# State-space layer: SiLUs behind an odd piece's first convolution, low gated values behind the last part's operands, output heads in alternating order

## The chip, the cores and the metric

The kernel runs on one core of a Trainium2 chip. The metric is the device time of the whole kernel in microseconds (us). Engines are called PE (TensorE), ACT (ScalarE), DVE (VectorE), POOL (GpSimd) and SP (SyncE). Each works through its own queue strictly in order, and they meet only at semaphores.

## What is computed

The reference is four stacked layers on 256 tokens (272 with 16 meta tokens) of width 1024. The change touches the mixer of the last one, a Mamba-2 state-space layer:

```python
proj = u @ w_in
z, xbc, dt = jnp.split(proj, [D_SSM, D_SSM + SSD_CONV_DIM], axis=-1)
xbc = jax.nn.silu(causal_dwconv(xbc, conv_w, conv_b))
...
y = ssd_chunked(front_pad(xs), front_pad(dt), a, front_pad(bs), front_pad(cs))[:, PAD:]
y = y + d_skip.astype(jnp.float32)[:, None] * xs
y = y.reshape(bsz, L, D_SSM) * jax.nn.silu(z.astype(jnp.float32))
yg = y.reshape(bsz, L, SSD_GROUPS, D_SSM // SSD_GROUPS)
yg = yg * lax.rsqrt(jnp.mean(yg * yg, axis=-1, keepdims=True) + EPS)
y = yg.reshape(bsz, L, D_SSM) * gate_norm.astype(jnp.float32)
return y.astype(u.dtype) @ w_out
```

There are 8 groups of 4 heads (head width 64, state 128). A group takes 4 tiles of 128 convolved channels (B, C and two of x) and 2 tiles of gate z.

## The kernel before

**Products.** Each weight is split into two f16 parts. SP loads a slot (two tiles of 128 columns) as f32; ACT writes its high part (`high_part`, L1538), DVE its low part (`low_part`, L2144), four slots ahead of use. In this layer each engine does half a slot behind each tile: tile j belongs to half (j-1) % 2. ACT signals `high_ready` only after the second half, so DVE's low part of a tile with an odd j waits until ACT has done the tile after it. A tile of the product is 24 matmuls (L690 to L692).

**Order of the layer's input product.** `mamba_pieces` deals the tiles into 16 pieces, two for each group g: piece s = 2g + k. Eleven tiles (j = 0 to 10) come before piece 0. Pieces 0 to 5 have two convolution tiles and a z tile; pieces 6 to 12 have two convolution tiles; pieces 13 to 15 have two z tiles. So the first tile of a piece has an even j in pieces 1, 3 and 5 and an odd j in pieces 7, 9, 11, 13, 14 and 15. In what follows A and B are the first and second tile of an odd piece, C and D those of the even piece after it.

- PE, odd piece: `first_outputs(g)` (L1423, L1424), `second_inputs(g)` (L1373 to L1364), A, `gate_sums` (L1446), B, a z tile if there is one. Even piece: `second_outputs(g-1)` (L1435 to L1437), `first_inputs(g)` (from L1384), C, `last_inputs(g)` (L1373 to L1398), D, a z tile if there is one. At the end `second_outputs(7)` and the product `out_m`, which waits for the release of all its four banks before it begins; the bank of tile 48 is one of them.
- ACT, odd piece: `second_exps` (L2069 to L2072), `silus` (a table load L2025, SiLU over the next group's four tiles L2028, SiLU over a pair of z tiles L2031 where one is due, a table load L2032), then for each tile its evacuation (L2019, for z L1524) and the high part (L1538), with `gate_squares` and `gate_root` (L2036, L2041, L2043) behind the first. Even piece: `first_exps` (L2057, L2059), `high_y` (L2047) where due, evacuation of C, `last_exps` (L2063 to L2065), `gate_squares`, evacuation of D. Pieces 14, 15 and the step after them (s = 16) call `silus` too, for the z pairs 5, 6 and 7.
- DVE: `outputs` (L2760), `weighted_x` (L2745), `scores` (L2751), low parts, three taps of each convolution (L2534), `gate_normed` (L2768), `low_y` (L2772).
- POOL, at even s: the gating y * silu(z) (L2974) of a pair that is due, which waits for that pair's SiLU; behind it `xw` (L2977), for which PE's `first_outputs` waits; `cd` (L2979); the squares' sum (L2983).

`GATES_AT` lists the steps s at which the pairs 0 to 7 are gated: 2, 4, 6, 8, 10, 14, 15, 16. `high_y` and `low_y` of a pair come two steps later. `first_inputs(g)` also waits for the `gate_root` of the piece before, since they share a bank.

Of the kernel before, what the change touches and what calls it, by code (L numbers as in the profile page):

```python
# [19 lines left out]
P = 128  # L20
# [12 lines left out]
META = 16  # L33
T = S + META
HD = 64
# [10 lines left out]
SSM_G = 8  # L46
SSM_HEADS = 32
SKIP = META - 2
REST = P + META
# [319 lines left out]
def two_stacks(nc, stream, small, params, consts, x_t, meta_t, out_t):  # L369
# [14 lines left out]
    with ExitStack() as ctx:  # L384
# [24 lines left out]
        def bank(b, lo=0, hi=512, rows=slice(0, P)):  # L409
            return psum[rows, b, lo:hi]  # L410
# [114 lines left out]
        xdt, xdt_c, xw = (sq_flat[:, 4 * HD * i:4 * HD * (i + 1)] for i in range(3))  # L525
# [156 lines left out]
        def _(pe):  # L682
# [665 lines left out]
            def mamba():  # L1348
                order, pieces = mamba_order(), mamba_pieces()
# [61 lines left out]
                def half_rows(h):  # L1411
                    return slice(64 * (h % 2), 64 * (h % 2) + 64)
# [13 lines left out]
                def second_outputs(g):  # L1426

                    pe.wait_ge(xdt_ready, 3 * g + 3)
                    pe.wait_ge(mt_ready, 3 * g + 3)
                    pe.wait_ge(y_out, 2 * g + 1)  # L1430
                    pe.wait_ge(prev_ready, g + 1)
                    pe.wait_ge(cd_ready, g + 1)
                    for h in range(4):
                        at, heads = (h // 2) * REST, slice(h * HD, h * HD + HD)
                        pe.matmul(bank(6, at, at + REST, half_rows(h)), xdt[:, heads], seg[:, h, :], start=True, stop=False)  # L1435
                        pe.matmul(bank(6, at + P, at + REST, half_rows(h)), xdt_c[0:META, heads], seg_c[0:META, h, :], start=False, stop=False)
                        mm = pe.matmul(bank(6, at, at + REST, half_rows(h)), prev[:, heads], cd[:, h, :], start=False, stop=True)  # L1437
                    mm.then_inc(y_done, 1)

                def gate_sums(g, s):  # L1440
# [75 lines left out]
        def _(act):  # L1516
# [481 lines left out]
            def mamba():  # L1998
# [89 lines left out]
                for s, piece in enumerate(pieces + [[], [], []]):  # L2088
                    g, k = divmod(s, 2)
                    if s < len(pieces):  # L2090
                        if k == 0:
                            first_exps(g)
                        else:
                            second_exps(g)
                    if s <= len(pieces) and (k or g + 1 >= SSM_G):
                        silus(g + 1 if k else SSM_G, range(gated, gates_in // 2))
                        gated = gates_in // 2
                    if s - 2 in GATES_AT:
                        high_y(GATES_AT.index(s - 2))
                    for i, (kind, _) in enumerate(piece):  # L2100
                        evac(j)
                        j += 1
                        gates_in += kind == "z"
                        if i == 0:
                            if k == 0:
                                last_exps(g)
                            gate_steps(s)
                    if not piece:
                        if s == len(pieces):
                            high_part(products["in_m"]["steps"][-1][0] + SPLIT)  # L2110
                        gate_steps(s)
# [20 lines left out]
        def _(dve):  # L2132
# [578 lines left out]
            def mamba():  # L2711
# [70 lines left out]
                for s, piece in enumerate(pieces + [[], [], []]):  # L2782
                    g, k = divmod(s, 2)
                    if 0 < s <= len(pieces):
                        outputs(s - 1)
                    if s < len(pieces):
                        weighted_x(3 * g + 2 * k, xdt, P, 2 * k)
                    if behind and k:
                        evac(behind)
                    if s < len(pieces):  # L2790
                        scores(3 * g + 2 * k, seg, P, REST if k else P)
                    if behind and not k:
                        evac(behind)
                    if behind:
                        behind_tile("in_m", behind)
                        behind = None
                    if s == len(pieces):
                        low_part(products["in_m"]["steps"][-1][0] + SPLIT)
                    if s - 2 in GATES_AT:
                        low_y(GATES_AT.index(s - 2))  # L2800
                    for i in range(len(piece)):
                        if i + 1 < len(piece):
                            evac(j)
                        if i == 0 and k == 0:
                            weighted_x(3 * g + 1, xdt_c, META, 3)
                            scores(3 * g + 1, seg_c, META, META)
                        if i + 1 < len(piece):
                            behind_tile("in_m", j)
                        else:
                            behind = j  # L2810
                        j += 1
                        if i == 0 and s - 1 in GATES_AT:
                            gate_normed(GATES_AT.index(s - 1))
                    if not piece and s - 1 in GATES_AT:
                        gate_normed(GATES_AT.index(s - 1))
# [321 lines left out]
```

## Time and profile before

| | |
|---|---|
| median of 3 runs | 1453.53 us (1453.22 to 1454.57) |
| profiled execution | 1452.95 us, its span 1451.2 us |
| PE busy | 1398.3 us (96%) |
| DVE busy | 1055.4 us (73%) |
| ACT busy | 833.0 us (57%) |
| POOL busy | 518.5 us (36%) |
| mean granted TensorE clock | 0.989 |

The profile is one execution. Times in its rows are us from the span's start, durations of one are in us in a timeline. The state-space layer's pieces run from about 1030 to 1211 us. A row of a timeline ends with the time for which the engine sat idle before it and what released it. The granted clock is given as a share: 1.00 is the 2.4 GHz level and 0.50 the 1.2 GHz level.

### The profile page before, as it was taken

The numbers are of one execution on the slowest core, as the hardware profiler recorded it, in microseconds if no ns is written. First come the engines' busy times: TensorE is split into PE (matmuls) and PEld (weight loads), VectorE is DVE, ScalarE is ACT, GpSimd is POOL, SyncE is SP. The second block draws the span as 40 slices with busy tenths as digits, with TensorE's granted clock in tenths as the row PEclk, the third lists the DMA queues.
The fourth block names the chain that finished last, engine by engine and source line by source line (L and its number), as shares of the span: only waits on it lengthen the run. The fifth ranks groups of instructions, "written<-read, shape, count | busy, mean of one in ns | idle before, by whom it ended". The sixth has DMA issues, their size and how long they took to land.

```text
span 1451.2 us, 29999 instructions
## 1 busy us (share of the span) xinstructions
PE 1398.3 (96%) x12859; PEld 1183.5 (82%) x12859; DVE 1055.4 (73%) x1361; ACT 833.0 (57%) x1253; POOL 518.5 (36%) x421
## 2 busy tenths in 40 slices
PE   8989999999899999999999999999999999999997
PEld 7778888888788888878678788887777778888886
DVE  5887986567797884567786888766667765898853
ACT  6575554337574453456885665545566777575552
POOL 0123995131047990234210366401212202146620
PEclk9989999999899999999999999999999999999998
DMA  9434466545323665525235355552533233556550
GB/s 369 172 117 146 148 212 213 191 163 182 127 100 117 231 206 203 189 88 189 93 133 212 137 200 180 189 193 88 174 113 121 86 107 118 200 185 206 189 177 30
DMA packets 35717, 235.61 MB, mean 162 GB/s; under 512 B 4736, under 2 KB 6784, under 8 KB 8832
## 3 DMA queue, kind: packets, MB, share of 16 engines
q1 hardware_dynamic: 35584, 233.68, 46.8%
q8 instruction: 102, 1.67, 0.5%
q14 instruction: 31, 0.25, 0.1%
HBM read 232.62 MB, written 1.05 MB: 161 GB/s over the span
## 4 chain that ended last, share of the span: by engine, by line
PE 76%; DVE 13%; ACT 7%; issue 2%; DMA 2%; SPq 0%; DVEq 0%; ACTq 0%
PE psum L690 23%; PE psum L692 23%; PE psum L691 23%; DVE low L2144 4%; PE psum L778 2%; DVE arena L2534 2%; ACT high L1538 2%; DMA raw<-stream 2%; ACT m L1891 1%; DVE m L2602 1%; PE psum L1044 1%; DVE arena L2605 1%; PE psum L1027 1%; ACT arena L2028 0%; ACT L2025 0%
## 5 line engine op out<-in xcount | busy, mean ns | idle before, releaser
L2144 DVE SCALAR_TENSOR_TENSOR low<-raw,high 128x2048 f16<-128x2048 f32 (+4 forms) x246 | 527.4, 2150 | 255.5 <-ACT high L1538 255.4
L690 PE MATMUL psum<-u,high 128*128 128x272 f16 (+3 forms) x2136 | 589.6, 276 | 14.7 <-DVE u L2445 5.4
L691 PE MATMUL psum<-u,high 128*128 128x272 f16 (+3 forms) x2136 | 589.1, 276 | 0.0
L692 PE MATMUL psum<-u,low 128*128 128x272 f16 (+3 forms) x2136 | 589.0, 276 | 0.0
L1538 ACT ACTIVATE high<-raw 128x2048 f16<-128x2048 f32 (+4 forms) x246 | 419.9, 1712 | 140.3 <-PE psum L692 125.8
L690 PE MATMUL psum<-arena,high 128*128 128x256 f16 (+2 forms) x1264 | 346.7, 274 | 2.8 <-ACT arena L1876 1.5
L692 PE MATMUL psum<-arena,low 128*128 128x256 f16 (+2 forms) x1264 | 346.6, 274 | 0.0
L691 PE MATMUL psum<-arena,high 128*128 128x256 f16 (+2 forms) x1264 | 346.6, 274 | 0.0
L690 PEld LDWEIGHTS psum<-u,high 128*128 128x128 f16 (+1 forms) x2136 | 209.9, 98 | 52.8 <-issue 15.6
L691 PEld LDWEIGHTS psum<-u,high 128*128 128x128 f16 (+1 forms) x2136 | 210.0, 98 | 31.1 <-issue 0.7
L692 PEld LDWEIGHTS psum<-u,low 128*128 128x128 f16 (+1 forms) x2136 | 209.8, 98 | 30.5
L2888 POOL TENSOR_TENSOR arena<-arena 128x256 f16<-128x256 f32 (+1 forms) x108 | 170.6, 1579 | 8.5
L2886 POOL TENSOR_TENSOR arena<-arena 128x256 f32<-128x256 f32 (+1 forms) x108 | 128.2, 1187 | 107.4 <-DVE arena L2550 105.7
L2534 DVE SCALAR_TENSOR_TENSOR arena<-psum,par,arena 128x271 f32<-128x271 f32 (+3 forms) x296 | 143.7, 492 | 23.3 <-ACT arena L2019 6.4
L690 PEld LDWEIGHTS psum<-arena,high 128*128 128x128 f16 x1264 | 123.7, 98 | 21.2 <-ACT arena L1876 1.8
L691 PEld LDWEIGHTS psum<-arena,high 128*128 128x128 f16 x1264 | 123.7, 98 | 18.4
L692 PEld LDWEIGHTS psum<-arena,low 128*128 128x128 f16 x1264 | 123.7, 98 | 16.5
L1524 ACT ACTIVATE arena<-psum 128x256 f32<-128x256 f32 (+3 forms) x138 | 51.7, 382 | 109.4 <-PE psum L692 68.8
L1839 ACT ACTIVATE arena<-psum,par 128x272 f32<-128x272 f32 (+1 forms) x88 | 49.4, 571 | 86.5 <-PE psum L692 85.0
L2896 POOL TENSOR_TENSOR m<-m,rstd 128x272 f32<-128x272 f32 (+1 forms) x12 | 9.0, 748 | 154.0 <-ACT rstd L1816 154.0
L2974 POOL TENSOR_TENSOR arena<-arena 128x516 f32<-128x516 f32 x8 | 11.2, 1395 | 117.3 <-DVE arena L2760 96.4
L2431 DVE TENSOR_TENSOR arena<-arena 128x256 f16<-128x256 f32 x64 | 48.4, 783 | 2.1 <-ACT arena L1524 2.1
(331 smaller groups left out, 1496.3 us busy)
## 6 DMA issues: line engine op xcount, KB each, us to landing
raw<-stream SPq DMA_DIRECT2D x208, 1024.0 KB, 4.8
raw<-stream SPq DMA_DIRECT2D x8, 768.0 KB, 4.2
raw<-stream SPq DMA_DIRECT2D x3, 896.0 KB, 5.1
con<-consts SPq DMA_DIRECT2D x1, 1758.0 KB, 16.7
raw<-stream SPq DMA_DIRECT2D x3, 512.0 KB, 3.5
h<-x_t SPq DMA_DIRECT2D x2, 512.0 KB, 6.2
out_t<-h SPq DMA_DIRECT2D x4, 256.0 KB, 2.1
misc<-small SPq DMA_DIRECT2D x1, 512.0 KB, 13.2
```

Source lines behind the costliest of these rows:

```text
L690: pe.matmul(out, w_hi, x[0], start=start, stop=False)
L691: pe.matmul(out, w_hi, x[1], start=False, stop=False)
L692: return pe.matmul(out, w_lo, x[0], start=False, stop=stop)
L778: return pe.matmul(bank(b, 0, n), C("mean", 0, P), x, start=start, stop=stop)
L1524: tell(act.activation(dst, bank(BANK[g], at, at + n, rows), func, scale=scale / W_SCALE), *evac_value(g))
L1538: tell(act.activation(high[:, at:at + w], raw[:, off:off + w], ACT.Copy, scale=W_SCALE), high_ready if half != 0 else None)
L1839: tell(act.activation(buf[:, i % GATED, 0:outputs], bank(BANK[g], ahead, ahead + outputs), ACT.Identity, scale=pcol(f"ffn_w{l}", 2 * 2 * F ...
L2144: tell(dve.scalar_tensor_tensor(low[:, at:at + w], raw[:, off:off + w], W_SCALE, high[:, at:at + w], ALU.mult, ALU.subtract), split_ready ...
L2431: tell(dve.tensor_tensor(f1_hi[:, t, :], f_relu[:, t % 4, :], f_relu[:, t % 4, :], ALU.mult), fh_ready)
L2534: ins = dve.scalar_tensor_tensor(dst[:, lo:outputs], bank(BANK[g], at, at + n), weight(taps_in_all - 1 - back), dst[:, lo:outputs], ALU.mu ...
L2886: tell(pool.tensor_tensor(tmp[:, t % 2, 0:n], a[:, t % depth, 0:n], b[:, t % depth, 0:n], ALU.mult))
L2888: tell(pool.tensor_tensor(lo[:, t, 0:n], tmp[:, t % 2, 0:n], hi[:, t, 0:n], ALU.subtract), f_ready)
```

## The change

Three edits, all in `mamba`. PE: in `second_outputs` the twelve products (each two instructions in the trace) are issued in two pairs of heads, the two heads of a pair alternating; the sums are the same. ACT: `silus` moves from ahead of the piece's tiles to behind the first tile's evacuation and high part (and behind `last_exps` in an even piece), for pieces 14 and 15 too; without a piece (s = 16) it stands behind `high_y`, which it preceded. DVE: `low_y`, where there is a piece, moves from ahead of C's taps to behind C's taps and the operands of the last part (`weighted_x` and `scores` of xdt_c, seg_c).

```diff
-                    for h in range(4):
-                        at, heads = (h // 2) * REST, slice(h * HD, h * HD + HD)
-                        pe.matmul(bank(6, at, at + REST, half_rows(h)), xdt[:, heads], seg[:, h, :], start=True, stop=False)
-                        pe.matmul(bank(6, at + P, at + REST, half_rows(h)), xdt_c[0:META, heads], seg_c[0:META, h, :], start=False, stop=False)
-                        mm = pe.matmul(bank(6, at, at + REST, half_rows(h)), prev[:, heads], cd[:, h, :], start=False, stop=True)
+                    for pair in ((0, 1), (2, 3)):
+                        at = (pair[0] // 2) * REST
+                        for h in pair:
+                            pe.matmul(bank(6, at, at + REST, half_rows(h)), xdt[:, h * HD:h * HD + HD], seg[:, h, :], start=True, stop=False)
+                        for h in pair:
+                            pe.matmul(bank(6, at + P, at + REST, half_rows(h)), xdt_c[0:META, h * HD:h * HD + HD], seg_c[0:META, h, :],
+                                      start=False, stop=False)
+                        for h in pair:
+                            mm = pe.matmul(bank(6, at, at + REST, half_rows(h)), prev[:, h * HD:h * HD + HD], cd[:, h, :], start=False, stop=True)
                     mm.then_inc(y_done, 1)
...
-                    if s <= len(pieces) and (k or g + 1 >= SSM_G):
-                        silus(g + 1 if k else SSM_G, range(gated, gates_in // 2))
-                        gated = gates_in // 2
                     if s - 2 in GATES_AT:
                         high_y(GATES_AT.index(s - 2))
+                    with_silus = s <= len(pieces) and (k or g + 1 >= SSM_G)
+                    if with_silus and not piece:
+                        silus(SSM_G, range(gated, gates_in // 2))
+                        gated = gates_in // 2
                     for i, (kind, _) in enumerate(piece):
                         evac(j)
                         j += 1
-                        gates_in += kind == "z"
                         if i == 0:
                             if k == 0:
                                 last_exps(g)
+                            if with_silus:
+                                silus(g + 1 if k else SSM_G, range(gated, gates_in // 2))
+                                gated = gates_in // 2
                             gate_steps(s)
+                        gates_in += kind == "z"
...
-                    if s - 2 in GATES_AT:
+                    if s - 2 in GATES_AT and not piece:
                         low_y(GATES_AT.index(s - 2))
                     for i in range(len(piece)):
...
                             weighted_x(3 * g + 1, xdt_c, META, 3)
                             scores(3 * g + 1, seg_c, META, META)
+                        if i == 0 and s - 2 in GATES_AT:
+                            low_y(GATES_AT.index(s - 2))
```

## Rows read from the trace of the kernel before

**Rows 1.** Windows: us, busy of PE, PEld, DVE, ACT, POOL; clock; DMA share; GB/s
```profile
1030.00:1213.00 183.00, 173.84 (x1578) 137.03 (x1577) 124.27 (x218) 124.08 (x200) 33.55 (x30) 0.99 0.34 113
1038.00:1039.00 1.00, 1.00 (x7) 0.70 (x6) 0.54 (x3) 0.77 (x3) 0.00 (x0) 0.50 0.99 418
80.00:85.00 5.00, 5.00 (x143) 3.99 (x142) 3.14 (x4) 4.11 (x12) 0.00 (x0) 0.67 0.69 228
85.00:92.00 7.00, 4.53 (x26) 3.27 (x23) 6.74 (x14) 2.50 (x5) 0.00 (x0) 0.50 0.73 272
```

**Rows 2.** Waits, 1030 to 1240 us: total us, times, longest us
```profile
DVE low L2144 <- ACT high L1538: 49.1, 17, 5.7
PEld psum L1436 <- issue: 6.3, 32, 0.2
PE psum L1373 <- DVE arena L2751: 7.0, 5, 2.7
```

**Rows 3.** Timeline of PE, pieces 5 and 6: start, us, engine, line
```profile
1101.45 0.60 PE L1446 MATMUL psum<-m,con 128*128 128x258 f32 x2
...
1115.55 0.20 PE L1373 MATMUL psum<-arena 128*16 128x16 f32 x2 [1.11 <-DVE arena L2751]
```

**Rows 4.** Timeline of ACT, piece 5
```profile
1100.75 1.28 ACT L2025 ACT_TABLE_LOAD   x1
...
1105.13 0.58 ACT L2019 ACTIVATE arena<-psum,par 128x272 f32<-128x272 f32 x1
...
1109.06 1.05 ACT L1538 ACTIVATE high<-raw 128x1024 f16<-128x1024 f32 x1
```

**Rows 5.** Timeline of DVE, piece 5
```profile
1106.69 1.23 DVE L2144 SCALAR_TENSOR_TENSOR low<-raw,high 128x1024 f16<-128x1024 f32 x1 [5.17 <-ACT high L1538]
...
1112.71 1.22 DVE L2144 SCALAR_TENSOR_TENSOR low<-raw,high 128x1024 f16<-128x1024 f32 x1
```

**Rows 6.** Timeline of ACT, piece 9 (two tiles)
```profile
1148.40 0.58 ACT L2019 ACTIVATE arena<-psum,par 128x272 f32<-128x272 f32 x1
...
1151.12 1.04 ACT L1538 ACTIVATE high<-raw 128x1024 f16<-128x1024 f32 x1
```

**Rows 7.** Timeline of DVE, piece 8 and the end of piece 9
```profile
1138.17 1.90 DVE L2772 TENSOR_TENSOR arena<-arena 128x516 f16<-128x516 f32 x1
...
1152.19 1.23 DVE L2144 SCALAR_TENSOR_TENSOR low<-raw,high 128x1024 f16<-128x1024 f32 x1 [1.61 <-ACT high L1538]
```

**Rows 8.** Timeline of PE: first matmul of `second_inputs` of groups 4, 5 and 6
```profile
1142.09 0.48 PE L1373 MATMUL psum<-arena 128*128 128x144 f32 x2 [1.02 <-DVE sq L2745]
...
1161.57 0.41 PE L1373 MATMUL psum<-arena 128*128 128x144 f32 x2
...
1182.34 0.48 PE L1373 MATMUL psum<-arena 128*128 128x144 f32 x2 [1.02 <-DVE sq L2745]
```

**Rows 9.** Timeline of ACT, pieces 14 and 15 and step 16
```profile
1193.91 1.28 ACT L2025 ACT_TABLE_LOAD   x1
...
1209.80 0.37 ACT L1524 ACTIVATE arena<-psum 128x258 f32<-128x258 f32 x1
...
1214.91 1.90 ACT L1538 ACTIVATE high<-raw 128x2048 f16<-128x2048 f32 x1
```

**Rows 10.** Timeline of POOL, piece 14: `xw`
```profile
1197.22 0.61 POOL L2977 TENSOR_TENSOR sq<-sq,arena 128x256 f32<-128x256 f32 x1
```

**Rows 11.** Timeline of PE, end of piece 14 to the start of `out_m`
```profile
1195.83 0.22 PE L1373 MATMUL psum<-arena 128*16 128x16 f32 x2
...
1199.70 0.66 PE L1423 MATMUL psum<-arena,sq 128*64 128x128 f32 x8
1200.28 0.70 PE L1424 MATMUL psum<-sq,arena 128*128 128x256 f32 x2
...
1207.85 0.46 PE L1435 MATMUL psum<-arena,sq 128*64 128x144 f32 x2
...
1210.67 0.28 PE L690 MATMUL psum<-arena,high 128*128 128x258 f16 x1
```

**Rows 12.** Timeline of DVE, step 16: low part of the fourth slot of `out_m`
```profile
1216.84 2.29 DVE L2144 SCALAR_TENSOR_TENSOR low<-raw,high 128x2048 f16<-128x2048 f32 x1 [1.98 <-ACT high L1538]
```

## Prediction

> **What bounds the kernel now.** The page says PE is busy 96% of the span, so the first view is the windows of the stage that the change touches: from 1030 to 1213 us PE is idle for 183.0 - 173.8 = 9.2 us [rows 1]. No reordering can win more there than this plus whatever PE work it removes. The second view is the waits: PE's largest is last_inputs (L1373) behind DVE's scores, 7.0 us in five waits, and DVE's own largest is its low part behind ACT's high part, 49.1 us [rows 2]. The third is the timelines of one round on three engines. The chain in piece 5 reads: ACT starts its SiLUs at 1100.75, although PE has tile A ready only at 1101.45 (gate_sums follows it); it reaches A at 1105.13 and ends the z tile's high part at 1109.06 + 1.05 [rows 3, 4]. DVE has sat 5.17 us for the high part that goes with A, and from there is busy without a break: the low part of B starts at 1112.71, and 2.8 us later PE's last_inputs is released, after an idle 1.11 us [rows 3, 5]. So DVE's late start, caused by ACT's order, is what PE waits for. Rounds of two-tile pieces are different. There the low part of A has an odd j and waits for the high part of B anyway (1152.19, behind ACT's 1151.12 + 1.04) [rows 6, 7], and what PE waits for is second_inputs, 1.02 us in two of three rounds, in which low_y took 1.90 instead of about 0.7 [rows 7, 8].
>
> **SiLUs behind A, pieces 1, 3 and 5.** ACT now waits for A: about 0.2 behind 1101.45, 0.9 later than its SiLUs start today. The work between is the same, so its last high part of the piece ends at 1110.11 + 0.9 = 1111.0. DVE's low part of the earlier tile starts four us sooner, its taps of A and B follow while ACT works, and its low part of B, which needs that last high part, starts at 1111.0 instead of 1112.71: 1.7 sooner. Everything from there to last_inputs is unchanged. That would release PE at 1113.85; C ends at 1115.55 - 1.11 = 1114.44 today and at 1113.5 with shorter output heads (below), so PE is still the earlier one. Three such rounds of the same pattern: **-5.1 us**. Of the 1.7, 1.1 is the idle time of today and 0.6 needs C to end sooner, which only the shorter heads bring.
>
> **SiLUs behind A, pieces 7, 9 and 11.** Here B's high part decides, and it is only delayed by ACT's wait for A. A loop forms: A ends, 0.2, ACT for 7.5 (evacuation and high part 1.4, SiLUs with two table loads 3.7, root 0.8, B 1.5), DVE for 3.5 (low part 1.1, gate_normed 0.8, outputs 0.55, weighted_x and scores 1.0), 0.1, PE for 9.1 (last_inputs 1.1, D 2.9, first_outputs 1.1, second_inputs 1.2, A 2.8): 20.4 us. Today a round from second_inputs to second_inputs is 19.5 (1142.09 to 1161.57) and 20.8 (1161.57 to 1182.34) [rows 8]. So the one round costs +1.0 and the other gains 0.4. The round before them (piece 7) enters from the three-tile regime: last_inputs is 0.9 later, but the 1.2 us around the wait at 1142.09 is gone, see low_y: -0.4. Together **+0.2 us**.
>
> **low_y behind the operands.** It no longer stands ahead of C's taps, so scores for second_inputs is ready up to 1.9 sooner. DVE then waits for D's high part in any case, and low_y fits in that wait of 1.3. This removes PE's two waits of 1.02, already used in the loop above. Nothing early waits for low_y itself (only out_m), so its own lateness costs nothing. Alone it is worth between 0 and -2.4.
>
> **Alternating heads.** second_outputs takes 1210.67 - 1207.85 = 2.82 us [rows 11]. The rows show heads of different halves running side by side: first_outputs, whose neighbours alternate, does eight instructions of 128 columns in 0.58 (1199.70 to 1200.28), and in second_outputs PE stalls 0.2 in front of each head's 16-row product (32 of them, 6.3 us) [rows 2, 11]. Alternating leaves 16 of these stalls and lets both long products overlap: 0.40 + 0.21 + 0.7 + 0.21 + 0.40 = 1.9, so 0.9 less for each group, 7.3 us in all; 0.4 if the short products don't overlap. On the path it is worth the 0.6 in each of three rounds that is counted above (C at 1113.5 instead of 1114.44, against DVE's 1113.85), and nothing elsewhere: in the other rounds C ends before DVE or ACT release what follows. The Trainium skill (TensorEngine Tiling (Array Packing), Key Properties) says that tiles of the array operate independently and that changing the mode drains the engine. By that rule each switch between 128 and 16 rows is a drain, and halving the switches would save about the amount above; the 0.2 us stalls agree. It changes nothing in the sum.
>
> **Piece 13** has z tiles: ACT waits 1.8 for its first tile, DVE's low part slips 1.9, and last_inputs(7) is bound by scores again. I take -0.3, between 0 and the heads' 0.9.
>
> **SiLUs in piece 14: a new wait.** POOL's gating waits for the SiLU of pair 5, and xw is queued behind it; PE's first_outputs(7) waits for xw. Today ACT starts that SiLU's table load at 1193.91, and xw is done at 1197.8, 1.9 ahead of PE's 1199.70 [rows 9 to 11]. Moved, the table load stands behind tile 45's evacuation, the whole of last_inputs (1195.83 + 1.13) and last_exps: 1195.83 + 1.13 + 0.2 + 0.8 = 1198.0, plus 1.28 + 0.63 of SiLU, 0.1, 1.24 of gating, 0.61 of xw, 0.1 = 1202.0. PE is ready at 1199.70: **+2.3 us**.
>
> **SiLUs in piece 15.** Today ACT evacuates tile 48 by 1209.80 + 0.37 = 1210.17, 0.5 ahead of out_m at 1210.67 [rows 9, 11], which waits for that bank. ACT's queue there is now: wait for tile 47 (it is ready at 1204.68), its evacuation and high part 1.2, SiLUs 3.2, squares and root 1.5, then tile 48. Counted from first_outputs(7), that bank is free 11.65 us on, against 10.97 today for out_m's start: **+0.7 us**; the 0.9 of shorter heads is lost in this wait.
>
> **Step 16.** high_y now stands ahead of silus and must wait for DVE's gate_normed, about 2.0 us behind tile 48's high part. That delays the fourth slot's high part (1214.91) and low part (done at 1219.05). Its margin: PE wants it 11.0 behind out_m's start, at 1221.7 [rows 9, 11, 12]. The margin of 2.6 is used up by 2.1 here and the rest of piece 15's lateness; I take 0, up to +0.5.
>
> **Sum.** -5.1 + 0.2 - 0.3 + 2.3 + 0.7 = -2.2 us. The profiled execution would go from 1452.95 to 1450.8, and the median, 0.6 above it, from 1453.53 to 1451.4. A measurement of this kernel can tell about 0.2%, 2.9 us, from no change; the forecast lies inside that.
>
> **Rivals.**
> *The tail waits don't arise* (chance 0.20): if POOL's xw or the bank of tile 48 has a slack that I misread, only the front counts: -5.1 to -5.3, 1448.4. Against it: both orders are fixed in the code and the margins are 1.9 and 0.5.
> *A short fall of the clock* (0.22): PE would idle 2.3 us ahead of first_outputs(7) and 1.6 ahead of out_m. After the longest wait of the stage, 2.7 us, the granted clock went from 1.00 to 0.50 (the 1.2 GHz level) [rows 1, 2] and about 3 us at it cost 1.4. After waits of 1.1 it did not. That gives -0.8, 1452.8.
> *Slower, by a long fall* (0.12): another fall held half clock through the 7 us of 85 to 92 and about a third of the 5 us before, some 10 us at half rate [rows 1]. If the waits in front of first_outputs(7) and out_m bring such a one while PE has nothing but out_m to do, it costs 5.1: +2.9 and more, 1456.5. It decides only if both waits come, since only then is PE twice idle in 10 us.
> *The heads don't overlap* (0.06), so the edit doesn't do what it says: second_outputs stays near 2.8. C would then be last in the three-tile rounds by 0.6 each: -0.4, 1453.1.
> *My forecast*: 0.40.
>
> The forecast's own range is 1450.4 to 1452.4. The 8-in-10 range leaves out the long fall and reaches the others: 1448.0 to 1454.0. Faster by over 0.2% takes the first rival and a third of the forecast, 0.34; slower 0.12; within 0.54.
>
> **What would show it.** Right: three low parts of DVE behind ACT at about 1 us instead of 5; last_inputs of groups 1 to 3 with idle time of 0.5 or less; L1435 to L1437 spanning 1.9 instead of 2.8; no idle before L1373 of second_inputs; an idle of about 2.3 before L1423 of group 7 put down to POOL's L2977, and one of 1.6 before out_m put down to ACT's L1524. Wrong: the round of piece 9 no longer than today, POOL's xw ahead of PE, or a granted clock of 0.50 near 1200.

## The result, and the profile after

| | before | after |
|---|---|---|
| median of 13 runs | 1453.8 us (1452.74 to 1455.38) | 1456.84 us (1452.0 to 1460.7) |
| profiled execution | 1452.95 us, span 1451.2 us | 1456.38 us, span 1454.6 us |
| mean granted clock | 0.989 | 0.986 |

The ratio is 1.002, 95% interval 1.0013 to 1.0027: the changed kernel is slower by about 3.0 us (1.9 to 3.9). The forecast was 1451.4, with 1448.0 to 1454.0 as its range. It was wrong in sign, and the time lies outside the range. One of the ten runs of experiment 7 took 2893.15 us; it is in no ratio, and without it the median there is 1452.79.

Lines have moved. ACT: L1538 is now L1542, L2019 is L2023, L2025 is L2029, L2031 is L2035, L1524 is L1528, and `gate_root`'s last line, L2043, is now L2047 (the number that `high_y` had before). DVE: L2144 is L2152, L2745 is L2753, L2751 is L2759. POOL: L2974 and L2977 are L2984 and L2987. PE's L1373, L1423 and L690 have kept their numbers, and L1435 to L1437 are now L1436 to L1441.

**Busy time.** The page of the changed kernel, each engine's busy time:

```profile
PE 1395.1 (96%) x12859; PEld 1181.5 (81%) x12859; DVE 1052.6 (72%) x1361; ACT 832.8 (57%) x1253; POOL 518.2 (36%) x421
```

PE is busy for 3.2 us less than before, and the kernel takes 3.4 us more in the profiled pair. So the alternating heads did remove work from the bounding engine. Where the time went is seen in the waits and in the clock.

**Waits.** PE, 1030 to 1250 us, changed kernel (total us, times, longest us):

```profile
PE psum L1373 <- DVE arena L2759: 7.5, 8, 2.7
PE psum L1384 <- ACT arena L2047: 4.5, 3, 1.9
PE psum L1423 <- POOL sq L2987: 2.4, 1, 2.4
PE psum L690 <- issue: 1.7, 1, 1.7
```

The third and the fourth row are the two tail waits of the forecast. The second is new and was not forecast: `first_inputs` of groups 4, 5 and 6 now waits for `gate_root` (ACT's L2047). ACT reaches it later, and PE is there sooner by its shorter heads. The first is the wait of [rows 2] for scores. It was 7.0 us in five waits and is now spread over eight. The waits at `last_inputs` of groups 1 to 3 fell from 1.27, 1.11 and 1.11 us to 0.67, 0.53 and 0.53. The 2.7 us of piece 0 is as before.

**The three-tile rounds.** ACT in piece 5, changed kernel (start, us, engine, line):

```profile
1099.59 0.58 ACT L2023 ACTIVATE arena<-psum,par 128x272 f32<-128x272 f32 x1 [0.93 <-PE psum L692]
...
1101.13 1.28 ACT L2029 ACT_TABLE_LOAD   x1
...
1108.02 1.05 ACT L1542 ACTIVATE high<-raw 128x1024 f16<-128x1024 f32 x1
```

DVE in the same piece:

```profile
1101.15 1.23 DVE L2152 SCALAR_TENSOR_TENSOR low<-raw,high 128x1024 f16<-128x1024 f32 x1 [1.69 <-ACT high L1542]
...
1109.10 1.23 DVE L2152 SCALAR_TENSOR_TENSOR low<-raw,high 128x1024 f16<-128x1024 f32 x1 [0.27 <-ACT high L1542]
```

Set them beside [rows 4, 5]. ACT now takes tile A first and the table load after it. DVE's wait for the first high part is 1.69 us instead of 5.17, and its second low part starts at 1109.10 instead of 1112.71, of which 2.06 us had been gained by the round before (the offset at `last_inputs` of group 2). Counted from PE's `second_inputs` of the same piece (1095.39 and 1097.45), ACT ends its last high part 1.02 us later than before and DVE starts 1.55 sooner.

**The tail, first wait.** ACT, POOL and PE around group 7's `first_outputs`, changed kernel:

```profile
1194.96 1.28 ACT L2029 ACT_TABLE_LOAD   x1
1196.25 0.63 ACT L2035 ACTIVATE arena<-arena 128x516 f32<-128x516 f32 x1
```

```profile
1197.03 1.27 POOL L2984 TENSOR_TENSOR arena<-arena 128x516 f32<-128x516 f32 x1 [18.92 <-ACT arena L2035]
1198.26 0.61 POOL L2987 TENSOR_TENSOR sq<-sq,arena 128x256 f32<-128x256 f32 x1
```

```profile
1199.13 1.12 PE L1423 MATMUL psum<-arena,sq 128*64 128x128 f32 x8 [2.38 <-POOL sq L2987]
...
1212.42 0.36 PE L690 MATMUL psum<-arena,high 128*128 128x258 f16 x1 [1.74 <-issue]
```

This is the forecast chain link by link: table load, SiLU of pair 5, gating, `xw`, and PE released 2.38 us late. The eight instructions of L1423 that follow then take 1.12 us, where in [rows 11] they took 0.66. That is the sign of the part that the forecast left out.

**The tail, second wait.** The profile names no releaser for the 1.74 us ahead of `out_m` ("issue"). The evacuation of tile 48 on ACT does fit:

```profile
1211.84 0.37 ACT L1528 ACTIVATE arena<-psum 128x258 f32<-128x258 f32 x1
```

It ends at 1212.21, and `out_m` starts 0.21 us later. In experiments 1, 6, 7 and 12 the two lie 0.20 us apart as well, whatever the wait was (0.58, 0.79, 1.74 and 0.80 us). In the kernel before, where `out_m` didn't wait, the distance is 0.50 [rows 9, 11].

**The clock.** Windows of the changed kernel: us, busy of PE, PEld, DVE, ACT, POOL; clock; DMA share; GB/s. The first is the stage of [rows 1], the next two are the stretch at the first tail wait, cut in two ways, then the one behind the second tail wait, and the last is one behind a wait of `first_inputs`:

```profile
1030.00:1213.00 183.00, 166.85 (x1568) 133.64 (x1567) 121.48 (x217) 122.61 (x199) 33.94 (x30) 0.98 0.34 113
...
1198.80:1202.20 3.40, 3.07 (x15) 2.52 (x16) 1.98 (x3) 1.38 (x3) 2.12 (x3) 0.50 0.00 0
1199.00:1203.00 4.00, 3.87 (x25) 3.26 (x26) 2.64 (x4) 1.57 (x3) 1.92 (x2) 0.60 0.00 0
1212.42:1216.72 4.30, 4.30 (x24) 3.19 (x25) 3.53 (x6) 2.19 (x3) 0.00 (x0) 0.60 0.00 0
1128.50:1134.00 5.50, 4.74 (x51) 3.65 (x49) 4.41 (x9) 3.94 (x7) 1.79 (x2) 1.00 0.00 0
```

At each tail wait the clock stands at the 1.2 GHz level for 3.4 us. The first of these stretches begins at 1198.8, before PE has started again at 1199.13; the second covers the first matmuls of `out_m`. The first tile of `out_m` shows the price: its 24 matmuls took 4.30 us instead of 2.65. The last stretch follows a wait of 1.94 us, and the clock stayed at 1.00.

**Where the 3.4 us are.** The offset of PE's marks, after less before, read from the two timelines of the profiled pair:

| up to | offset then | this stretch |
|---|---|---|
| end of `second_inputs` of group 0 (1048 us) | +1.0 | +1.0, in the start of the kernel |
| `last_inputs`, groups 1, 2, 3 | -3.60 | -1.55, -1.52, -1.54 |
| `second_inputs`, groups 4, 5, 6 | -2.85 | -0.17, +1.11, -0.19 |
| `last_inputs`, group 7 | -2.99 | -0.14 |
| `first_outputs`, group 7 | -0.57 | +2.42, the wait for `xw` |
| start of `out_m` | +1.75 | +2.32: 1.45 of slow clock up to the heads, 0.87 of wait (1.74 less what the heads got shorter) |
| end of `out_m`'s first tile | +3.40 | +1.65 of slow clock |

From there on the offset doesn't change. The +1.0 at the start belongs to no edit. It comes from a fall of the clock at about 31 us that the one profiled execution has and the other lacks, as a window of each shows, first of before, then of after:

```profile
20.00:45.00 25.00, 22.12 (x192) 18.73 (x192) 16.84 (x25) 16.01 (x24) 1.83 (x4) 1.00 0.91 350
```

```profile
20.00:45.00 25.00, 22.32 (x182) 18.61 (x183) 17.05 (x24) 16.30 (x24) 1.73 (x4) 0.93 0.90 350
```

Nine of the twelve profiled executions below have it, whatever they change (not experiments 1, 7 and 11), and the one of before has not. No edit reaches that place, and PE waits there in all of them, before first, then after:

```profile
31.96 0.27 PE L690 MATMUL psum<-u,high 128*128 128x256 f16 x1 [2.88 <-ACT arena L1524]
```

```profile
31.86 0.37 PE L690 MATMUL psum<-u,high 128*128 128x256 f16 x1 [2.66 <-ACT arena L1528]
```

More than this differs ahead of the stage: the first `last_inputs` starts at 1036.31 us in experiment 7, at 1036.68 in the kernel before, at 1037.77 in the changed one and at 1039.04 in experiment 6. So marks are to be compared within the stage, and whole times by their medians.

### The profile page after: what moved, and what is told of

It is laid out like the page before. It is cut to its first block, busy times and chain, and to the rows that moved or that the text cites. A ratio compares the mean times of both kernels' runs of the same rounds, so it can differ in the third digit from the quotient of the medians.

```text
span 1454.6 us, 29999 instructions
## 1 busy us (share of the span) xinstructions
PE 1395.1 (96%) x12859; PEld 1181.5 (81%) x12859; DVE 1052.6 (72%) x1361; ACT 832.8 (57%) x1253; POOL 518.2 (36%) x421
## 4 chain that ended last, share of the span: by engine, by line
PE 78%; DVE 10%; ACT 8%; issue 2%; DMA 2%; POOL 0%; SPq 0%; DVEq 0%; ACTq 0%; POOLq 0%
PE psum L690 23%; PE psum L691 23%; PE psum L692 23%; DVE low L2152 3%; PE psum L778 2%; ACT high L1542 2%; DMA raw<-stream 2%; ACT m L1895 1%; ACT L2029 1%; DVE m L2610 1%; ACT arena L2032 1%; PE psum L1044 1%; DVE arena L2542 1%; DVE arena L2613 1%; PE psum L1027 1%
## 5 line engine op out<-in xcount | busy, mean ns | idle before, releaser
L2152 DVE SCALAR_TENSOR_TENSOR low<-raw,high 128x2048 f16<-128x2048 f32 (+4 forms) x246 | 527.0, 2148 | 265.0 <-ACT high L1542 264.8
L690 PE MATMUL psum<-u,high 128*128 128x272 f16 (+3 forms) x2136 | 590.1, 276 | 14.5 <-DVE u L2453 5.5
L1542 ACT ACTIVATE high<-raw 128x2048 f16<-128x2048 f32 (+4 forms) x246 | 419.9, 1712 | 140.2 <-PE psum L692 125.7
L690 PE MATMUL psum<-arena,high 128*128 128x256 f16 (+2 forms) x1264 | 347.5, 275 | 4.6 <-issue 1.7
L690 PEld LDWEIGHTS psum<-u,high 128*128 128x128 f16 (+1 forms) x2136 | 210.1, 98 | 52.8 <-issue 15.7
L690 PEld LDWEIGHTS psum<-arena,high 128*128 128x128 f16 x1264 | 123.9, 98 | 23.3 <-issue 2.9
L1528 ACT ACTIVATE arena<-psum 128x256 f32<-128x256 f32 (+3 forms) x138 | 51.6, 381 | 115.9 <-PE psum L692 69.3
L2984 POOL TENSOR_TENSOR arena<-arena 128x516 f32<-128x516 f32 x8 | 10.2, 1279 | 122.3 <-DVE arena L2768 89.1
```

The source lines that it names most:

```text
L690: pe.matmul(out, w_hi, x[0], start=start, stop=False)
L1528: tell(act.activation(dst, bank(BANK[g], at, at + n, rows), func, scale=scale / W_SCALE), *evac_value(g))
L1542: tell(act.activation(high[:, at:at + w], raw[:, off:off + w], ACT.Copy, scale=W_SCALE), high_ready if half != 0 else None)
L2152: tell(dve.scalar_tensor_tensor(low[:, at:at + w], raw[:, off:off + w], W_SCALE, high[:, at:at + w], ALU.mult, ALU.subtract), split_ready ...
```

## The experiments

The theory: the forecast's moves of work are right, and the two tail waits, with a fall of the clock behind each, cost more than the front brings. Rivals: the waits alone are to blame, the front brings less than its marks say, or the shorter heads themselves do harm. "Changed kernel" is the one with all three edits. Each time is a median beside the kernel before of the same job: 1454.13, 1454.02 and 1454.18 us in the three jobs. Ratios are to that kernel. `due` stands for the condition under which SiLUs are called. Filler matmuls write a bank that nobody reads at that time.

### 1. The tail put back

```diff
-                    with_silus = s <= len(pieces) and (k or g + 1 >= SSM_G)
-                    if with_silus and not piece:
-                        silus(SSM_G, range(gated, gates_in // 2))
-                        gated = gates_in // 2
+                    due = s <= len(pieces) and (k or g + 1 >= SSM_G)
+                    with_silus = due and s < 13
+                    if due and not with_silus:
+                        silus(g + 1 if k else SSM_G, range(gated, gates_in // 2))
+                        gated = gates_in // 2
                     if s - 2 in GATES_AT:
                         high_y(GATES_AT.index(s - 2))
```

> The changed kernel with the SiLUs of pieces 13, 14, 15 and of step 16 back at their old place (ahead of the piece's tiles, ahead of high_y at step 16). Theory (the front wins about 5 us and the tail gives it back, by the waits at first_outputs(7) and out_m and the two falls of the granted clock behind them): 4.5 to 5.5 us faster than before, ratio 0.9965, no idle time in front of first_outputs(7), no half clock from 1190 us on. Rival (the loss sits in the longer loop of the two-tile pieces or is spread over the kernel): no faster than before.

Measured: 1447.84 us, ratio 0.9959 (0.9947 to 0.9972), 6.3 us below before (4.5 to 5.5 was expected) and 9 below the changed kernel. Window of it, and its first matmul of `out_m`:

```profile
1045.00:1240.00 195.00, 185.58 (x1759) 151.71 (x1759) 136.16 (x232) 142.00 (x224) 36.53 (x30) 1.00 0.36 123
```

```profile
1205.57 0.27 PE L690 MATMUL psum<-arena,high 128*128 128x258 f16 x1 [0.58 <-issue]
```

The clock is whole from 1045 us to the end of the layer, and `out_m` starts 6.85 us earlier than in the changed kernel (1212.42), of which 1.0 lies ahead of the stage. So the loss sits in the SiLUs of pieces 13 to 15 and step 16: the two waits and the clock behind them. The front as changed is a gain.

### 2. The two waits filled with work

```diff
                 def first_outputs(g):
+                    if g == SSM_G - 1:
+                        keep_awake(7, 20)
...
                 second_outputs(SSM_G - 1)
+                keep_awake(5, 14)
```

> The changed kernel, with PE doing 20 products of 256 columns that nobody reads in front of first_outputs(7) and 14 in front of out_m, some 2.2 and 1.5 us, inside its two waits. The waits for POOL and ACT stay. Theory (each wait is followed by a fall of the granted clock that costs about 1.5 us more): clock 1.00 throughout 1190 to 1230 us, and about 3 us faster than the changed kernel, 0 to 2 us faster than before. Rival (only the waits cost, the clock adds nothing): the same time as the changed kernel, about 3 us slower than before.

Measured: 1452.7 us, ratio 0.9992 (0.9983 to 1.0001). Timeline of PE at the first wait, and the window:

```profile
1196.65 2.35 PE L720 MATMUL psum<-con 128*128 128x256 bf16 x20
1199.20 0.66 PE L1425 MATMUL psum<-arena,sq 128*64 128x128 f32 x8 [0.20 <-POOL sq L2990]
```

```profile
1045.00:1240.00 195.00, 185.07 (x1752) 150.75 (x1750) 131.90 (x226) 138.04 (x217) 35.56 (x30) 1.00 0.35 117
```

PE starts `first_outputs` no earlier (1199.20 against 1199.13) and idles only 0.20 us. Its eight instructions again take 0.66 us, the clock is 1.00, and the kernel is 4 us faster than the changed one by the medians, 3.0 by the two profiled executions (1453.38 against 1456.38). The waits are still paid here, so this prices the falls alone. The rival that the waits alone are to blame is out. It holds for more than the one execution in the profile: the mean granted clock over all runs is 0.9883 here and 0.9854 in the changed kernel, and one stretch of 3.4 us at half rate is worth 0.0012 of it.

### 3. The SiLUs moved in pieces 1, 3 and 5 only

The other two edits stay.

```diff
-                    with_silus = s <= len(pieces) and (k or g + 1 >= SSM_G)
+                    due = s <= len(pieces) and (k or g + 1 >= SSM_G)
+                    with_silus = due and s in (1, 3, 5)
```

> The changed kernel with the SiLUs behind the first tile in pieces 1, 3 and 5 only; low_y and the output heads as changed. Theory (only a first tile with an even j has a low part waiting for its own high part, so the move pays in these three and costs 0.9 us a round in pieces 7, 9 and 11): 8 to 9 us faster than before, and 3 to 4 faster than the kernel with only the tail as before. Rival (the two-tile rounds lose nothing by the move): the same as that kernel, 5 us faster than before.

Measured: 1445.58 us, ratio 0.9942 (0.993 to 0.9955), 8.6 us below before. It is 2.3 faster than with the tail put back, where 3 to 4 was expected, since experiment 1 had come out faster than forecast. The two differ only in pieces 7, 9 and 11, so that is what the move costs there: a round takes 19.6 us here (`last_inputs` at 1133.23, 1152.81 and 1172.40) and 20.6 in the changed kernel.

### 4. The heads alone

Only the edit of `second_outputs`, on the kernel before.

```diff
-                    for h in range(4):
+                    for pair in ((0, 1), (2, 3)):
...
+                        for h in pair:
+                            mm = pe.matmul(bank(6, at, at + REST, half_rows(h)), prev[:, h * HD:h * HD + HD], cd[:, h, :], start=False, stop=True)
```

> The kernel before with the alternating output heads alone. Theory (second_outputs falls from 2.82 to 1.9 us, 7.3 us of PE work in all, but nearly everywhere DVE or ACT release what follows): 1 to 2 us faster. Rival (PE bounds the stage, so PE work removed is time removed): 6 to 7 us faster.

Measured: 1457.14 us, ratio 1.002 (1.0011 to 1.0029). Both sides had expected a gain, and it is a loss of 3 us by an edit that only takes PE work away. Waits of PE, 1045 to 1240 us, then the first of them in the timeline, then the four us behind each:

```profile
PE psum L1373 <- DVE arena L2755: 7.6, 6, 2.2
```

```profile
1066.11 0.20 PE L1373 MATMUL psum<-arena 128*16 128x16 f32 x2 [2.22 <-DVE arena L2755]
```

```profile
1067.00:1071.00 4.00, 4.00 (x25) 2.90 (x24) 2.33 (x6) 1.32 (x4) 3.04 (x3) 0.57 0.64 195
1094.00:1098.00 4.00, 4.00 (x30) 2.89 (x29) 3.87 (x7) 1.32 (x4) 3.41 (x3) 0.57 0.49 145
1121.00:1125.00 4.00, 3.93 (x29) 2.80 (x30) 3.93 (x6) 1.32 (x4) 3.40 (x4) 0.59 0.38 92
```

PE reaches `last_inputs` 0.95 us sooner, DVE releases it when it did before, so waits of 1.27, 1.11 and 1.11 us grow to 2.22, 2.06 and 2.06. Behind each of the three the clock falls, and the next tile takes 4.2 to 4.3 us instead of 2.78. Over all runs the mean granted clock is 0.9853, against 0.9881 for the kernel before. Theory so far: a saving in front of a fixed wait lengthens the wait, and the longer wait costs the clock. Experiment 9 tests it.

### 5. low_y alone

```diff
-                    if s - 2 in GATES_AT:
+                    if s - 2 in GATES_AT and not piece:
                         low_y(GATES_AT.index(s - 2))
...
+                        if i == 0 and s - 2 in GATES_AT:
+                            low_y(GATES_AT.index(s - 2))
```

> The kernel before with low_y behind the last part's operands alone. Theory (it removes PE's two waits of 1.02 us at second_inputs of groups 4 and 6, but ACT's and DVE's next steps start from tile D, which doesn't move, so part of each comes back at the next last_inputs): 1 to 2 us faster. Rival (an unrelated wait takes their place at once): no change. Other rival (the full 2.4 us).

Measured: 1451.63 us, ratio 0.9984 (0.9975 to 0.9993), a gain of 2.4 us. Waits of PE at L1373, 1045 to 1240 us:

```profile
PE psum L1373 <- DVE arena L2751: 4.3, 4, 1.3
```

Those on DVE's L2745 [rows 8] are gone and nothing came in their place. The gain is the upper bound that the prediction gave, and the expectation's 1 to 2 us were too low: the rival had it. The medians alone don't separate the two (the interval reaches from 1.0 to 3.6 us), but the marks do. In the profiled pair the stage gives 2.2 us: the first `last_inputs` stands 2.13 us late against the kernel before, the end of the span 0.1 early.

### 6. The changed kernel with the heads in turn

Only `second_outputs` is put back.

```diff
-                    for pair in ((0, 1), (2, 3)):
+                    for h in range(4):
```

> The changed kernel with the output heads in their old order. Theory (PE reaches each wait 0.9 us later, so the waits of 1.7 us ahead of out_m and of 0.5 at last_inputs shrink, and the fall of the granted clock behind out_m's wait stays away, 1.6 us): the wait ahead of out_m 0.8 us, clock 1.00 behind it, and a time within 1.5 us of the changed kernel, either way. Rival (the heads' 7.3 us of PE work are worth something like that on the path): 4 us or more slower than the changed kernel.

Measured: 1455.31 us, ratio 1.0006 (0.9997 to 1.0015), 1.5 to 1.8 us faster than the changed kernel, with 7.6 us more work for PE (0.95 in each of eight groups). The expectation had the second fall staying away, and both did. PE at group 7's `first_outputs`, its wait ahead of `out_m`, and the window:

```profile
1201.58 0.66 PE L1423 MATMUL psum<-arena,sq 128*64 128x128 f32 x8 [2.38 <-POOL sq L2983]
```

```profile
PE psum L690 <- issue: 0.8, 1, 0.8
```

```profile
1045.00:1240.00 195.00, 187.60 (x1709) 150.50 (x1707) 130.68 (x222) 136.89 (x216) 35.52 (x30) 1.00 0.34 114
```

The same wait of 2.38 us brought no fall here. So a wait's length alone doesn't decide. Over all runs the mean granted clock is 0.9881, against 0.9854 for the changed kernel.

### 7. The SiLUs of piece 14 put back

The other pieces keep theirs where the change put them.

```diff
+                    due = s <= len(pieces) and (k or g + 1 >= SSM_G)
+                    with_silus = due and s != 14
+                    if s == 14:
+                        silus(SSM_G, range(gated, gates_in // 2))
+                        gated = gates_in // 2
```

> The changed kernel with the SiLU of piece 14 alone back at its old place. Theory (xw stands behind the gating that waits for this SiLU, 2.4 us of wait at first_outputs(7), and the clock falls behind it, 1.5 us): no wait at first_outputs(7), clock 1.00 there, 3 to 4 us faster than the changed kernel; the wait ahead of out_m stays at 1.5 us or more. Rival (ACT, not POOL's order, is late in any case): less than 1 us faster.

Measured: 1452.95 us, ratio 0.9989 (0.998 to 0.9999), some 4 us below the changed kernel. Windows ahead of and behind the start of `out_m`, and the wait there:

```profile
1190.00:1207.00 17.00, 14.50 (x145) 11.50 (x142) 6.84 (x13) 13.57 (x24) 6.95 (x6) 1.00 0.37 125
1207.00:1211.00 4.00, 3.96 (x21) 2.92 (x22) 3.19 (x6) 1.89 (x3) 0.00 (x0) 0.57 0.00 0
```

```profile
PE psum L690 <- issue: 1.7, 1, 1.7
```

Without the wait for `xw` the first fall is gone, which pays for the wait and the fall (2.4 + 1.4). The wait of 1.74 ahead of `out_m` and its own fall stay. Each fall follows its own wait.

### 8. As 3, with the first wait of the stage filled

```diff
+                        if s == 0 and i == 0:
+                            pe.wait_ge(b_ready, 1)
+                            keep_awake(7, 24)
                         if i == 0 and k == 0:
                             last_inputs(g)
```

> The kernel with the SiLUs behind the first tile in pieces 1, 3 and 5 only (low_y and heads as changed), and in PE's wait of 2.75 us at last_inputs of group 0, which all kernels have, 24 products of 256 columns that nobody reads, 2.6 us. Theory (the fall of the granted clock behind this wait costs 1.4 us): clock 1.00 from 1030 to 1230 us, 1.4 us faster than without the products, some 10 us faster than before. Rival (the products delay last_inputs, or the clock falls elsewhere instead): no faster than without them.

Measured: 1443.26 us, ratio 0.9926 (0.9914 to 0.9939), 2.3 below experiment 3 (1.4 was expected; the intervals of the two ratios touch) and 10.8 below before (computed 1454.18 x 0.0074): the fastest of all. The fall of [rows 1] at 1038 is gone:

```profile
1022.00:1240.00 218.00, 211.49 (x1996) 173.32 (x1995) 155.05 (x263) 157.50 (x247) 44.35 (x38) 1.00 0.40 135
```

### 9. The heads alone, with their three waits filled

```diff
                 def last_inputs(g):
+                    if g in (1, 2, 3):
+                        pe.wait_ge(b_ready, g + 1)
+                        keep_awake(7, 16)
```

> The kernel with the alternating heads alone, and in PE's waits at last_inputs of groups 1, 2 and 3 (2.2, 2.1 and 2.1 us in that kernel) 16 products of 256 columns that nobody reads, 1.8 us. Theory (heads alone are 3 us slower because each longer wait is followed by a fall of the granted clock, 1.4 us each): clock 1.00 from 1045 to 1230 us, 4 us faster than heads alone, 1 to 2 us faster than before. Rival (the order of the heads itself costs the time): as slow as heads alone.

Measured: 1452.39 us, ratio 0.9988 (0.9979 to 0.9997), 4.7 us below experiment 4 and 1.7 below before.

```profile
1045.00:1240.00 195.00, 187.72 (x1773) 152.65 (x1771) 134.79 (x225) 138.97 (x218) 36.62 (x30) 1.00 0.34 117
```

Three falls of about 1.5 us make 4.5, so the whole loss of experiment 4 is the clock's. The mean granted clock over all runs rose from 0.9853 to 0.9891. What the shorter heads save by themselves is 1.7 us (0.4 to 3.1) of the 7.6 that PE no longer works.

### 10. The kernel before, with only the first wait filled

The filler matmuls of 8, on the kernel before.

> The kernel before with the same 24 products in its wait of 2.74 us at last_inputs of group 0. Theory: the stage's one fall of the granted clock goes, 1.4 us faster. Rival (some other part of the stage takes it back): no change.

Measured: 1452.47 us, ratio 0.9988 (0.9979 to 0.9997), 1.7 us below before. The clock is 1.00 over 1030 to 1240 us. A fall can be bought back with matmuls that compute nothing.

### 11. The SiLUs of pieces 1, 3 and 5 alone

On the kernel before, with `with_silus = due and s in (1, 3, 5)` and neither of the other edits.

> The kernel before with the SiLUs behind the first tile in pieces 1, 3 and 5 alone; heads and low_y as before. Theory (DVE would release last_inputs 1.7 us sooner a round, but C ends only 1.1 to 1.3 sooner than last_inputs starts now): no wait at last_inputs of groups 1 to 3, 3.3 to 4 us faster. Rival (the move works only together with shorter heads): less than 1.5 us faster.

Measured: 1450.18 us, ratio 0.9974 (0.9964 to 0.9983), a gain of 3.8 to 4.0 us. No wait is left at `last_inputs` of groups 1 to 3: the 3.5 us of waits, and a little more. The parts now add up: 3.8 here, 2.4 for low_y and 1.7 for the heads with a whole clock make 7.9, and the three together gave 8.6 in experiment 3.

### 12. The SiLUs as changed, alone

The ACT edit in full, without low_y and the heads.

```diff
-                    if s <= len(pieces) and (k or g + 1 >= SSM_G):
-                        silus(g + 1 if k else SSM_G, range(gated, gates_in // 2))
+                    with_silus = s <= len(pieces) and (k or g + 1 >= SSM_G)
...
+                            if with_silus:
+                                silus(g + 1 if k else SSM_G, range(gated, gates_in // 2))
```

> The kernel before with the SiLU edit as it is in the change, alone. Theory (front -3.5, longer loop in the two-tile pieces +2 since low_y still stands in the way, wait for xw +2.4, wait ahead of out_m +0.8): within 2.5 us of before, rather slower. Rival (without the alternating heads the edit is a gain, and the loss of the change is the heads'): 2.5 us or more faster.

Measured: 1459.75 us, ratio 1.0038 (1.0026 to 1.0051), 5.6 us slower, the slowest of all. Within 2.5 us was expected. The wait of PE at `second_inputs`, 1045 to 1240 us:

```profile
PE psum L1373 <- DVE sq L2749: 3.1, 3, 1.0
```

low_y in its old place holds `second_inputs` back in all three two-tile rounds, where two had it before, and the rounds from group to group take 21.86 us each instead of 19.5 and 20.8 [rows 8]. That is 43.72 us for two rounds instead of 40.25, so +3.5: the wait behind low_y and the later SiLUs stand in one loop, and their prices add up. By PE's marks within the stage the front gives -2.7, these two rounds +3.5, the wait for `xw` +2.4, the wait ahead of `out_m` +0.9 and the fall behind it +1.7, which is 5.7 in all. In the full change low_y's move takes this away: with it the same SiLUs stand at 1455.31 (experiment 6). The wait of 2.38 us for `xw` again brought no fall; one of 0.80 ahead of `out_m` did:

```profile
1215.00:1220.00 5.00, 4.21 (x24) 3.12 (x24) 3.42 (x6) 2.90 (x5) 0.33 (x1) 0.66 0.01 3
```

In experiment 6 one of 0.79 at the same place brought none.

## Why the prediction was wrong, step by step

**SiLUs in pieces 1, 3 and 5: right.** -4.6 us against -5.1. Each round gave 1.54 instead of 1.7: DVE's release sets it, and ACT's last high part came 1.02 us later instead of 0.9. Of PE's wait 0.5 to 0.7 remains, where 0.35 was implied (1113.85 against 1113.5). Experiment 11 shows that the edit alone empties those waits.

**Two-tile pieces: right in mechanism, a little too good.** +0.75 against +0.2, in the pattern that the loop gave: -0.17, +1.11, -0.19 against -0.4, +1.0, -0.4. The loop is 20.6 us long instead of 20.4. The forecast did not see `first_inputs`' wait for `gate_root` (4.5 us in three waits), since it followed DVE's side only. It costs nothing there: behind each of the three, PE still waits 0.76 us for DVE at the next `last_inputs`.

**low_y: right.** Both waits went; alone it is worth 2.4, the upper bound, by the medians and 2.2 by the marks.

**The heads overlap: right, and their value was the blind spot.** 2.82 us became 1.87 (1081.02 to 1082.89) against 1.9. The Trainium skill (TensorEngine Tiling (Array Packing), Key Properties) says that tiles work independently and that a change of mode drains the engine, and the trace agrees: the weight load's stalls of 0.2 us at the 16-row products went from 32 to 16 (6.3 to 3.2 us), and with both long products side by side that took off 0.95 for each group. "On the path it is worth the 0.6 in each of three rounds, and nothing elsewhere" treated idle time as free. Experiments 4 and 9 show that it isn't: the same edit is -1.7 us with its waits filled and +3.0 with them empty. The rival that called the edit void (0.06) is out; that it could do harm was in none of the cases.

**Piece 13: right**, -0.14 against -0.3.

**The two tail waits: right.** 2.42 against 2.3. Ahead of `out_m` 0.87 net of the heads against 0.7. Step 16 stayed at 0: the offset is constant behind `out_m`'s first tile, and in experiment 2, where no fall gives DVE more time, no new wait of PE appears there either.

**The clock: the step that failed.** In the profiled pair the terms without it come to -4.6 + 0.75 - 0.14 + 2.42 + 0.87 = -0.7, 1.5 off the forecast's -2.2 in five small pieces. The two falls add 1.45 + 1.65 = 3.1, the one at the start 1.0, and the sum is the +3.4 seen. The likeliest case put the clock at nothing behind two new waits of 2.3 and 1.6 us, and experiments 2, 1 and 7 show that this is the step that failed. The rival on the clock had the price right, 1.4 against 1.45 and 1.65, and the places too, but it allowed one fall and a chance of 0.22. The slower case asked for a long fall, of which there was none. Two short ones at 1.4 would have given -2.2 + 2.8 = +0.6, and with the other terms as they came +2.1: "slower" needed no rival of its own, only the second wait counted like the first. The rows held the hint: a fall behind 2.7 us, none behind 1.1, and 2.3 and 1.6 lie between. The text took the middle as safe, where no row bore that out. Nor was 2.7 us a sure sign: the trace of before itself has a wait of 2.88 us, at 31.96, with no fall behind it.

**What is open** is why some of these waits bring a fall and others don't. The table has the evidence, one profiled execution for each kernel:

| wait, us | where | fall |
|---|---|---|
| 2.44 to 2.93 | at 32 us, all fourteen kernels, reached by no edit | yes in ten, no in four |
| 2.7 | piece 0, each kernel that doesn't fill it | yes |
| 2.38 | group 7's `first_outputs`, changed kernel | yes |
| 2.38 | the same place, experiments 6 and 12 | no |
| 2.22, 2.06, 2.06 | `last_inputs` 1 to 3, heads alone | yes |
| 1.94 | `first_inputs` 4, changed kernel and experiments 1, 2 and 7 | no |
| 1.74 | ahead of `out_m`, changed kernel and experiment 7 | yes |
| 0.80, 0.79 | ahead of `out_m`, experiments 12 and 6 | yes, no |
| 0.58 | ahead of `out_m`, experiments 1, 3 and 4 | no |
| 1.27 and less | `last_inputs` 1 to 3, kernel before | no |

Length helps to sort them and doesn't decide. The first row shows that the place doesn't either: it is the same wait in the same code, with a fall behind it in some executions (from 2.44 us on) and none in others (up to 2.88). So part of it changes from one execution to the next, and a single profile can't say how often a fall comes. The spread of the changed kernel's runs fits: the two slowest (1460.6 and 1460.7) have a mean granted clock of 0.980, the fastest (1452.0) of 0.988. What sets it wasn't found, and no kernel was profiled several times.

## What to carry to other kernels

Idle time of the bounding engine is not free: before work is taken out of the stretch ahead of a wait that something else sets, add up how long the wait becomes, and price one fall of the clock (here 3.4 us at half rate, 1.4 to 1.65 us), as a chance and not as a certainty, for each wait that grows past those that the profile shows to be harmless. Where such a wait can't be removed, matmuls that nobody reads gave 1.7 and 2.3 us in one wait, 4 in two and 4.7 in three. And an edit that is good in one regime (SiLUs behind the first tile where three tiles cover them) is to be applied only there: by itself it was worth -3.8 us in pieces 1, 3 and 5, and +5.6 everywhere.

## What the runs showed of the hardware

In the state-space stage waits of 0.8 to 2.7 us, in a stream that is 96% busy, were each followed, in seven of the places above, by some 3.4 us at the 1.2 GHz level, and in others of the same length by none. The kernel in which PE did 7.6 us more work was the faster one (1455.31 against 1456.84 us). One wait that no edit reaches, 2.44 to 2.93 us long at 32 us from the start, had such a stretch behind it or at its end in ten of fourteen profiled executions, at a cost of about 1.1 us (clock 0.93 instead of 1.00 in the same 25 us). Each group of 16-row products between 128-row ones stalled the weight load for 0.2 us (32 stalls and 6.3 us before, 16 and 3.2 after).
